# A decoder step on one core: mixer heads overlapped, memory projections moved forward, output projection restaged

## The chip, the core and the metric

The kernel runs on one core of a Trainium2 chip, as one program. A core has TensorE (PE in the profile; its weight loads are PEld), VectorE (DVE), ScalarE (ACT), GpSimd (POOL) and SyncE (SP), each with its own list of instructions worked off in order, and DMA queues that SP, ACT and POOL feed. SBUF holds the operands, PSUM takes the results of TensorE. Engines wait for each other by semaphores. The metric is the device time of one execution in microseconds (us).

## The reference, cut to what matters

One inference step of a one-layer decoder, all float32, for a prompt of 512 tokens and for 8 samples of one token each, width 1024:

```python
z = rms_norm(x) @ w_in                      # all projections at once
# group A, 4 heads of 128: mLSTM
s   = (q @ k.T) * exp(logd - m_t)           # decay
num = g_inter * (C @ q) + s @ v
den = g_inter * (n @ q) + sum(s)
h   = num / max(abs(den), exp(-m_t))
C_new = g_prev * C + (w_s * v).T @ k        # p_c; s_c for the samples
y_m = sigmoid(o) * rms_norm(h)
# group B, 4 heads of 128: sparse attention over the selected keys
y_a = softmax(q @ k_sel.T) @ v_sel
# memory: 256 tokens
mem_k = rms_norm(rms_norm(mem) @ w_ck);  mem_v = rms_norm(mem) @ w_cv
x = x + concat(y_m, y_a) @ w_out
q = rms_norm(rms_norm(x) @ w_cq)            # cross-attention
x = x + (softmax(q @ mem_k.T) @ mem_v) @ w_co
x = x + conv_ffn(rms_norm(x))               # up, conv, GELU gate, down
```

The samples take their state C (8 x 4 x 128 x 128), their keys and values (by page table) and their memory keys and values from caches.

## The kernel before, in words

**Products.** Each float32 product is made of three: weights and activations are split into a high part, as TensorE reads it, and the low rest. For every 128 output columns of weights (a tile) SP loads `raw` (512 KB), ACT casts it to `whi` (L831, or `act_split`), POOL subtracts to `wlo` (L845 and L1626, the low part), and PE runs high by high, high by low and low by high over eight k-blocks of 128. There are two slots `s`, for even and odd tiles; each buffer of a slot is free when the stage behind it is done (`raw_full`, `hi_full`, `split_full`, `w_used`, `out_free` are the semaphores, counted over all stages by `BASE`).

**Order.** Every engine's list is written out by hand, stage after stage: input projection, attention of the prompt, indexer of the samples, then the stretch that is changed here:

1. *Four mLSTM heads* (`pe_ml`, `act_ml`, `vec_ml`). For a head, PE spreads the running maxima over the partitions (`pe_ml_rows`), makes four score blocks (L1203), and numerator and denominator by key block (`pe_ml_nd`). ACT makes the decay of each block (L1268, L1270), DVE multiplies it in (L1309: 512, 384, 256, 128 columns). DVE makes the gate's column and `wv` (L1313, L1314), from which PE builds the new state; ACT copies it out (L1280, L1282) and stores it (`p_c`). DVE takes the denominator (L1321, L1322), ACT inverts it by log and exp (L1284, L1285), DVE makes `hb` (L1324), ACT squares it (L1289), PE sums over the head (L1245, a product with ones), ACT takes the root (L1292, L1293) and the output gate (`sg_e`, L1275 to L1277), and DVE scales by both (L1330, L1331: the two gate steps). Between these lie two samples' key products each head: PE spreads a sample's query row (L1058) into bank 2 or 3, DVE multiplies it with the gathered keys (L1065) and sums (L1069). All scores and sample rows go through the two banks 2 and 3; `p_c`, the maxima and the mean square through banks 0 and 1.
2. *The samples' softmax* (`satt_soft`, L1073 to L1102) and their gates (L1385 to L1411), small operations in turn.
3. *The state loop* over 8 samples b (`pe_mls`, `vec_mls`, `act_mls_store`, `sync_mls`). SP loads the state of b into one of two buffers `cb` once the store of b-2 has landed. PE spreads two rows of b (L1368), makes memory tile 2b (L912), the sample's attention value (`pe_satt_v`, L1112) and memory tile 2b+1. A memory tile is 128 columns of w_ck (tiles 0 to 7) or w_cv (8 to 15) over 256 memory tokens; `act_mem_tile` copies it out and casts the weights of two tiles on, PE transposes it back (`pe_mem_back`, L920). DVE updates the state, and ACT stores it (`out_s_c`). After the loop come the splits of y for the projection (`act_split_ml`, `vec_split_y`), the samples' mean square, and the sample part of y.
4. *Output projection* (`pe_out_proj`): x is transposed in (`pe_turn_in`), 8 tiles are made in pairs, each added to x by DVE (`vec_residual`, L1686). DVE normalises the memory keys (`vec_mem_norm`, four operations over all 2048 columns, with ACT's root between; L1731 and L1732 are the last two), PE transposes them (`pe_mem_keys`). ACT squares x (L1632), PE sums the squares (L249). `act_cache` starts 4 MB of cached memory keys and the stores of `p_mem_k` and `p_mem_v` from ACT's queue.
5. *Norm and query*: DVE writes the scaled x into one of two buffers `hs2`, ACT takes the high part from it, DVE the low part (L274), and PE starts the query tiles (`pe_fused`) k-block by k-block as the low parts come.

Behind that follow cross-attention, up, conv, down, which the change leaves alone. SP's order in the loop, which the change leaves as it is:

```python
for b in range(B):
    if b == 2: sync_reload(sp)
    if b >= 2:
        for t in (2 * b, 2 * b + 1): sp_weights(sp, t)
        sp.wait_ge(sc_stored[b % 2], 16 * (b // 2))
    else: sp.wait_ge(ym_ready, H)
    sp.dma_start(cb[:, b % 2], ...)          # state of sample b
```

and ACT's handing over of a memory tile: `act_mem_tile(t)` waits for PE's tile t, copies it to `kvT`, and then casts the weights of tile t + 2; `act_mem_step(t)` runs `act_mem_out` of t - 1 and `act_mem_tile` of t.

## Time and profile before

| what | value |
|---|---|
| median of 3 runs (lowest to highest) | 1365.85 us (1362.71 to 1368.11) |
| the profiled execution: its own time | 1363.25 us |
| its span in the profile | 1361.5 us |
| its mean granted clock | 0.90 |
| PE busy | 1139.3 us, 84% |
| DVE busy | 587.4 us, 43% |
| ACT busy | 486.0 us, 36% |
| POOL busy | 401.0 us, 29% |
| chain that ended last | PE 68%, DVE 15%, ACT 6%, issue 6%, DMA 2% |

The profile is of one execution; all its times are within the span, counted from the span's start. Busy time leaves out waits. The granted clock is TensorE's, as a part of full speed. The chain is followed back from the last instruction, at each step to what released it. "Issue" is time in which the engine waited for nothing that the profile shows. In the rows, a line is an operation with its start, its time, the line of the code, output and inputs, and in brackets how long its engine had been idle and what released it.

### The profile page before, as it was taken

What the parts mean: (1) busy time and instruction counts of PE and PEld (TensorE: products, weight loads), DVE (VectorE), ACT (ScalarE), POOL (GpSimd) and SP (SyncE); (2) the same over time, 40 slices, a digit from 0 to 9 for tenths busy, and PEclk for the clock granted to TensorE, in tenths of its full rate; (3) what the DMA queues carried; (4) which work ended last, traced back from release to release, by engine and by line L of the source; (5) the groups of instructions that cost most, each with busy time, mean ns of one, the idle gap of its engine ahead of it and who ended that gap; (6) DMA issues with size and microseconds to landing.
All of it is one profiled execution on the core that took longest, in us unless ns stands there. A gap on an engine that the chain in (4) does not pass through costs nothing.

```text
span 1361.5 us, 20030 instructions
## 1 busy us (share of the span) xinstructions
PE 1139.3 (84%) x7911; PEld 1000.9 (74%) x7911; DVE 587.4 (43%) x1105; ACT 486.0 (36%) x870; POOL 401.0 (29%) x200
## 2 busy tenths in 40 slices
PE   4788967657884586797687999988999999999998
PEld 4788857657873242686677986652999999998997
DVE  3405486886566566454513124552333334430000
ACT  5222242333244254123013454231355555543212
POOL 2212211122120112275121314540244444443442
PEclk9977788789897687799798999997899999999999
DMA  5223211113220112465161211844133332223222
GB/s 141 63 51 78 63 32 31 47 57 84 68 73 0 49 48 82 139 196 178 31 232 47 63 47 34 311 166 139 47 92 93 92 92 88 87 86 91 85 85 90
DMA packets 165331, 121.82 MB, mean 89 GB/s; under 512 B 7383, under 2 KB 154421, under 8 KB 164974
## 3 DMA queue, kind: packets, MB, share of 16 engines
q1 hardware_dynamic: 149536, 96.35, 23.6%
q10 hardware_dynamic: 12848, 14.08, 3.1%
q0 software_dynamic: 2880, 10.49, 2.7%
q8 instruction: 43, 0.70, 0.2%
q14 instruction: 24, 0.20, 0.0%
HBM read 111.81 MB, written 9.27 MB: 89 GB/s over the span
## 4 chain that ended last, share of the span: by engine, by line
PE 68%; DVE 15%; ACT 6%; issue 6%; DMA 2%; POOL 1%; ACTq 1%; DVEq 0%; POOLq 0%; SPq 0%
PE PS L237 43%; PE PS L912 3%; PE PS L1879 3%; PE PS L387 2%; DMA raw<-in_w_out 1%; PE PS L1368 1%; PE PS L2332 1%; ACT ikc L470 1%; PE PS L1839 1%; PE PS L1825 1%; DVE rw L314 1%; DVE tk L581 1%; PE PS L1112 1%; PE PS L953 1%; DVE tiny L580 1%
## 5 line engine op out<-in xcount | busy, mean ns | idle before, releaser
L237 PE MATMUL PS<-ahi,whi 128*128 128x260 f32 (+1 forms) x1456 | 311.9, 297 | 26.5 <-POOL wlo L2720 9.9
L1626 POOL TENSOR_TENSOR wlo<-raw,whi 128x1024 fp32r<-128x1024 f32 x84 | 201.0, 2393 | 415.9 <-ACT whi L831 415.9
L237 PE MATMUL PS<-alo,whi 128*128 128x260 f32 (+1 forms) x1456 | 302.1, 290 | 0.0
L237 PE MATMUL PS<-ahi,wlo 128*128 128x260 f32 (+1 forms) x1456 | 301.5, 290 | 0.0
L237 PEld LDWEIGHTS PS<-ahi,whi 128*128 128x128 f32 (+1 forms) x1456 | 235.1, 197 | 31.8 <-issue 18.1
L237 PEld LDWEIGHTS PS<-alo,whi 128*128 128x128 f32 (+1 forms) x1456 | 233.8, 196 | 0.0
L237 PEld LDWEIGHTS PS<-ahi,wlo 128*128 128x128 f32 (+1 forms) x1456 | 233.0, 195 | 0.0
L831 ACT CAST whi<-raw 128x1024 fp32r<-128x1024 f32 x108 | 113.1, 1048 | 317.0 <-PE PS L237 295.1
L2720 POOL TENSOR_TENSOR wlo<-raw,whi 128x1024 fp32r<-128x1024 f32 (+1 forms) x31 | 73.2, 2361 | 293.0 <-ACT whi L2758 293.0
L2459 DVE SCALAR_TENSOR_TENSOR PS<-ub,cw,PS 128x512 f32<-128x512 f32 x44 | 33.2, 755 | 156.0 <-ACT PS L2437 156.0
L237 PE MATMUL PS<-gHi,whi 128*128 128x260 f32 x352 | 71.1, 283 | 0.0
L237 PE MATMUL PS<-gHi,wlo 128*128 128x260 f32 x352 | 70.8, 282 | 0.0
L237 PE MATMUL PS<-gLo,whi 128*128 128x260 f32 x352 | 70.7, 282 | 0.0
L845 POOL TENSOR_TENSOR wlo<-raw,whi 128x1024 fp32r<-128x1024 f32 x18 | 43.1, 2394 | 61.2 <-ACT whi L831 61.0
L2551 DVE TENSOR_TENSOR xT<-xT,PS 128x520 f32 x8 | 5.6, 697 | 123.0 <-PE PS L237 123.0
L237 PEld LDWEIGHTS PS<-gLo,whi 128*128 128x128 f32 x352 | 54.3, 188 | 0.0
L237 PEld LDWEIGHTS PS<-gHi,whi 128*128 128x128 f32 x352 | 54.2, 188 | 0.1
L237 PEld LDWEIGHTS PS<-gHi,wlo 128*128 128x128 f32 x352 | 54.2, 188 | 0.0
L2758 ACT CAST whi<-raw 128x1024 fp32r<-128x1024 f32 (+1 forms) x31 | 32.1, 1037 | 57.3 <-PE PS L237 56.6
L1033 POOL DMA_INDIRECT skv<-in_cache_k,rowT x16 | 15.4, 962 | 102.1 <-DVE rowT L1021 55.3
L912 PE MATMUL PS<-hmhi,whi 128*128 128x256 f32 x128 | 38.6, 301 | 0.0
L912 PE MATMUL PS<-hmhi,wlo 128*128 128x256 f32 x128 | 37.2, 291 | 0.0
(502 smaller groups left out, 1870.7 us busy)
## 6 DMA issues: line engine op xcount, KB each, us to landing
raw<-in_w_up SPq DMA_DIRECT2D x44, 512.0 KB, 3.8
raw<-in_w_in SPq DMA_DIRECT2D x30, 512.0 KB, 3.8
ckv<-in_cache_mem_v SPq DMA_DIRECT2D x8, 1024.0 KB, 5.4
raw<-in_w_down SPq DMA_DIRECT2D x16, 448.0 KB, 3.8
raw<-in_w_ck SPq DMA_DIRECT2D x8, 512.0 KB, 4.5
raw<-in_w_cv SPq DMA_DIRECT2D x8, 512.0 KB, 4.3
raw<-in_w_out SPq DMA_DIRECT2D x8, 512.0 KB, 4.1
ckv<-in_cache_mem_k ACTq DMA_DIRECT2D x4, 1024.0 KB, 10.6
```

The lines of the kernel that those rows point to most:

```text
L237: ins = nc.tensor.matmul(out[0:m, half, 0:HALF], w[:, s, k, 0:m], x[:, k0 + k, half * HALF:(half + 1) * HALF], start=(first and k == 0 and ...
L314: V(nc.vector.tensor_tensor(t1[:, :, a], x[:, :, a], cos, ALU.mult))
L387: m = nc.tensor.matmul(bank[:, j:j + H], ikc[:, p0:p0 + 4, :].rearrange("d a r -> d (a r)"), iqS[:, :, b], start=True, stop=True)
L831: nc.scalar.copy(whi[:, s], raw[:, s]).then_inc(hi_full[s], 1)
L845: nc.gpsimd.tensor_tensor(wlo[:, s], raw[:, s], whi[:, s].bitcast(F32), ALU.subtract).then_inc(split_full[s], 1)
L912: m = nc.tensor.matmul(PJ[1][:, s, 0:NMEM], w[:, s, k, :], x[:, k, :], start=(k == 0 and j == 0), stop=(k == KT - 1 and j == 2))
L1033: nc.gpsimd.indirect_dma_start(skv[:, b % 2, t, :], None, table, bass.IndirectOffsetOnAxis(ap=rowT[:, t, b:b + 1], axis=0)).then_inc(skv_f ...
L1626: nc.gpsimd.tensor_tensor(wlo[:, s], raw[:, s], whi[:, s].bitcast(F32), ALU.subtract).then_inc(split_full[s], 1)
L1879: m = nc.tensor.matmul(PJ[o][:, half, 0:2 * P], w[:, k, o * P:(o + 1) * P], x[:, 4 * part + k, half * 2 * P:(half + 1) * 2 * P], start=(k ...
L2459: V(v.scalar_tensor_tensor(c, ub[:, s, r, 1:1 + SEQ], cw[:, 1, f:f + 1], c, ALU.mult, ALU.add))
L2720: g.tensor_tensor(wlo[:, s, :, 0:w], raw[:, s, :, 0:w], whi[:, s, :, 0:w].bitcast(F32), ALU.subtract).then_inc(split_full[s], 1)
L2758: a.copy(whi[:, s, :, 0:w], raw[:, s, :, 0:w]).then_inc(hi_full[s], 1)
```

## The change

Three edits in one. **Heads overlapped:** the next head's rows and first two scores stand ahead of this head's mean-square product on PE; on ACT the next head's gate column and first decay block stand ahead of this head's root, the output gate's three steps between the decay blocks, the copies of the state behind the denominator, and `p_c`'s store later still; on DVE the next head's first decay product stands ahead of this head's gate steps, and the sample's product apart from its sum. The sample rows move from banks 2 and 3 to PJ[1], with a semaphore of their own. **Memory tiles 0 to 2** go to the sample softmax and gates, the state loop starts with tile 3 and spreads the rest by a table; POOL's gathers and low parts follow the same order; the memory keys are squared on ACT in the turns of samples 4 and 5 and scaled on DVE in that of 6; the samples' attention value and root come earlier in the tail. **Output projection and norm:** the first half of the first output tile starts with the attention part of y as the low parts come; x is turned in in two halves with the first output tiles between; key transposes and squares stand in other places; the cache loads wait for the other slot; the norm has eight buffers; and PE runs the high products of both first query tiles ahead of the low ones.

The diff, cut to its core (waits and semaphores of moved code left out):

```diff
@@ pe_satt_k
-            nc.tensor.matmul(pe_bank(pe, 2 + b % 2)[:], rowsel[:, b, :], sw[:], ...)
+            if b < 2: pe.wait_ge(hm_lo, 4)
+            else:     pe.wait_ge(k_used, 2 * (b - 1))
+            nc.tensor.matmul(PJ[1][:, b % 2, :], rowsel[:, b, :], sw[:], ...).then_inc(k_row, 1)
@@ pool_mixers
-            for b in range(B):
-                for t in (2 * b + 2, 2 * b + 3):
-                    pool_weights(pool, t)
-                if b + 2 < B:
-                    pool.wait_ge(v_used, b + 1)
-                    gather("cache_v", b + 2)
+            for t in (2, 3, 4):
+                pool_weights(pool, t)
+            for b in range(2, B):
+                pool.wait_ge(v_used, b - 1)
+                gather("cache_v", b)
+                for t in (2 * b + 1, 2 * b + 2):
+                    pool_weights(pool, t)
+            pool_weights(pool, 17)
@@ pe_ml
             pe_ml_nd(pe, h, 0)
+            pe_satt_k(pe, 2 * h)
             pe_ml_score(pe, h, 2)
...
+            if h < H - 1:
+                pe_ml_rows(pe, h + 1)
             pe_satt_k(pe, 2 * h + 1)
             if h < H - 1:
-                pe_ml_rows(pe, h + 1)
+                pe_ml_score(pe, h + 1, 0)
+                pe_ml_score(pe, h + 1, 1)
             pe.wait_ge(hsq_ready, h + 1)
             nc.tensor.matmul(pe_bank(pe, 0)[:], ones[:], hsq[:], ...)
@@ act_ml, the new order
+            act_ml_decay(act, h, 1)
+            sg_e = exp(-z); sg_e = ln(sg_e + 1)
+            act_ml_decay(act, h, 2)
+            sg_e = exp(-sg_e)
+            act_ml_decay(act, h, 3)
+            dn = ln(dn); dn = exp(-dn)
+            cst = copy(bank 0); nst = copy(bank 1)
+            if h < H - 1: act_ml_m(act)
+            hsq = square(hb)
+            if h < H - 1: act_ml_em(act)
+            act.dma_start(O["p_c"][0, 0, h], cst[:, h % 2])
+            if h < H - 1: act_ml_first(act, h + 1)   # gate column, decay block 0
+            act_ml_root(act)
@@ vec_ml, the new order
+            vec_ml_decay(dve, h, 1); wcol, wv
+            vec_satt_k(dve, 2 * h)
+            vec_ml_decay(dve, h, 2); vec_ml_decay(dve, h, 3)
+            vec_satt_sum(dve, 2 * h)
+            dn (two steps); sg_s; hb
+            if h < H - 1: vec_ml_m(dve, h + 1)
+            vec_satt_k(dve, 2 * h + 1)
+            if h < H - 1: vec_ml_decay(dve, h + 1, 0)
+            vec_satt_sum(dve, 2 * h + 1)
+            y (two gate steps)
@@ pe_mls, act_mls_store
+        ROW_TILES = [(3,), (4, 5), (6, 7), (8, 9), (10, 11), (12, 13), (14,), (15,)]
-                pe_mem_step(pe, 2 * b)
+                pe_mem_step(pe, ROW_TILES[b][0])
                 pe_satt_v(pe, b)
-                pe_mem_step(pe, 2 * b + 1)
+                for t in ROW_TILES[b][1:]:
+                    pe_mem_step(pe, t)
...
-                for t in (2 * b, 2 * b + 1):
+                for t in ROW_TILES[b]:
                     act_mem_step(act, t)
+                if b in (4, 5):
+                    act_key_squares(act, b - 4)     # 4 squares, the root at 5
                 act.wait_ge(sc_in, b + 1)
                 act.dma_start(O["s_c"][0, b]..., cb[:, b % 2])
@@ vec_mls, vec_key_norm
+                if b == 6:
+                    vec_key_norm(dve)               # 8 products of 256 columns
@@ pe_mixers
+            pe.wait_ge(k_used, 2 * B)
+            pe_mem_step(pe, 0)
             pe_satt_soft(pe)
+            pe_mem_step(pe, 1)
+            pe_satt_turn(pe)
+            pe_mem_step(pe, 2)
             pe_mls(pe)
@@ act_mixers
+            act_mem_step(act, 1)
             act_satt_soft(act)
+            act_mem_step(act, 2)
             act_mls_first(act)
...
             act_mem_tile(act, 15)
+            act_satt_v(act)
+            act_mls_last(act)
             act_mem_out(act, 15)
             act_split_ml(act)
@@ pe_out_proj
+            pe_out_first(pe)       # half 0 over k = 4..7, 0..3 as y_lo comes, then half 1
+            pe_turn_in(pe, 0, 4)
+            pe_out_tile(pe, 0, 1)
+            pe_turn_in(pe, 4, KT)
+            for i in range(1, 4):
+                pe_out_tile(pe, i, 0)
+                for f in (2 * i - 2, 2 * i - 1):
+                    pe_sumsq(pe, 1, f, sq2, T)
+                if i == 3:
+                    pe_mem_keys(pe, 0, 4)
+                pe_out_tile(pe, i, 1)
+            pe_sumsq(pe, 1, 6, sq2, T)
+            pe_mem_keys(pe, 4, 6)
+            pe_sumsq(pe, 1, 7, sq2, T)
+            pe_mem_keys(pe, 6, KT)
@@ act_out_proj
             for i in range(4):
                 if i:
                     for f in (2 * i - 2, 2 * i - 1):
                         act_squares(act, 1, f)
+                act_split(act, 0, BASE["out"][0] + i + 1)
+                if i == 3:
+                    act_squares(act, 1, 6)
+                act_split(act, 1, BASE["out"][1] + i + 1)
                 if i == 1:
                     act_cache(act)
@@ act_cache
-            act.wait_ge(out_free[0], BASE["out"][0] + 1)
+            act.wait_ge(out_free[1], BASE["out"][1] + 1)
@@ pe_query_first, ahead of the loop of pe_fused, which now starts at n = 2
+            for k in range(KT):
+                pe.wait_ge(nhi_ready, KT + k + 1)
+                for s in range(2): for w in (whi, wlo): for half in range(2):
+                    nc.tensor.matmul(PJ[s][:, half, 0:HALF], w[:, s, k, :], ahi[:, k, ...], ...)
+            for k in range(KT):
+                pe.wait_ge(nlo_ready, KT + k + 1)
+                for s in range(2): for half in range(2):
+                    nc.tensor.matmul(PJ[s][:, half, 0:HALF], whi[:, s, k, :], alo[:, k, ...], ...)
```

## Rows read from the trace of the kernel before

**Rows 1.** Windows by stage: us, busy time of each engine (instructions), granted clock, DMA share, GB/s
```profile
459.30:540.40 81.10, 64.63 (x204) 31.34 (x203) 50.35 (x80) 41.36 (x80) 18.01 (x19) 0.84 0.24 68
540.40:553.20 12.80, 1.68 (x7) 1.25 (x7) 9.87 (x34) 0.81 (x3) 0.00 (x0) 0.50 0.61 209
553.20:637.60 84.40, 84.40 (x574) 71.77 (x574) 35.07 (x41) 24.04 (x45) 50.20 (x27) 0.94 0.55 169
637.60:691.00 53.40, 35.31 (x237) 32.79 (x236) 24.90 (x31) 8.67 (x18) 9.47 (x4) 0.78 0.15 43
691.00:730.20 39.20, 33.07 (x224) 30.18 (x224) 6.67 (x13) 6.39 (x9) 9.48 (x4) 0.91 0.61 215
730.20:755.70 25.50, 18.57 (x115) 16.34 (x116) 11.72 (x17) 11.93 (x20) 4.74 (x2) 0.93 0.14 41
```

**Rows 2.** Windows, two halves of the third head, DVE alone: us, busy, clock, DMA
```profile
502.70:514.59 11.89, 6.30 (x11) 1.00 0.18 51
514.59:522.01 7.42, 6.29 (x10) 0.54 0.24 70
```

**Rows 3.** Timeline of the third head: start, us, engine, line, operation
```profile
508.53 1.22 DVE L1065 TENSOR_TENSOR kprod<-skv,PS 128x1024 f32<-128x1024 f32 x1 [1.44 <-PE PS L1058]
509.90 1.22 DVE L1069 TENSOR_REDUCE tiny<-kprod 128x8 f32<-128x1024 f32 x1
...
512.40 0.69 DVE L1322 SCALAR_TENSOR_TENSOR dn<-PS,dn 128x512 f32<-128x512 f32 x1
...
514.59 0.69 DVE L1324 TENSOR_TENSOR hb<-PS,dn 128x512 f32<-128x512 f32 x1 [1.50 <-ACT dn L1285]
...
516.00 2.07 PE L1245 MATMUL PS<-hsq,ones 128*128 128x512 f32 x2 [2.31 <-ACT hsq L1289]
...
517.86 3.19 PE L1203 MATMUL PS<-z_m 128*128 128x512 f32 x4
```

**Rows 4.** Timeline, the gates' first operation, the first state row, and a cast
```profile
544.38 0.15 DVE L1385 TENSOR_TENSOR s<-gt,sm 8x4 f32<-8x4 f32 x1
...
553.16 3.78 PE L1368 MATMUL PS<-s_tok,rowsel 8*128 8x512 f32 x4 [1.68 <-DVE Qb L1411]
...
592.90 1.05 ACT L831 CAST whi<-raw 128x1024 fp32r<-128x1024 f32 x1
```

**Rows 5.** Timeline, the memory keys' last two operations and the output tile behind them
```profile
668.65 2.34 POOL L1626 TENSOR_TENSOR wlo<-raw,whi 128x1024 fp32r<-128x1024 f32 x1 [3.37 <-ACT whi L831]
669.12 4.02 DVE L1731 TENSOR_TENSOR mk_t<-mk_t,xc 128x2048 f32<-128x2048 f32 x1 [8.37 <-ACT xc L1744]
...
673.18 2.29 DVE L1732 TENSOR_TENSOR mk_t<-mk_t,ckg 128x2048 f32<-128x2048 f32 x1
...
676.65 0.77 PE L237 MATMUL PS<-ahi,whi 128*128 128x260 f32 x2 [9.21 <-DVE xT L1686]
```

**Rows 6.** Chain that ended last, pieces in order of time: start, us, what
```profile
556.94 5.42 PE PS L912 x24
...
584.53 2.92 PE PS L912 x24
587.45 1.91 PE PS L1368 x4
...
592.60 1.68 PE PS L1112 x16
...
694.62 17.27 DMA raw<-in_w_out
```

**Rows 7.** DMA issues in the state loop: output and input, queue, count, size, median us to land
```profile
raw<-in_w_cv SPq DMA_DIRECT2D x8, 512.0 KB, 4.3
out_s_c<-cb ACTq DMA_DIRECT2D x8, 256.0 KB, 5.1
```

**Rows 8.** Timeline, an ACT activation that also sums its row (cross-attention)
```profile
766.11 0.56 ACT L1956 ACTIVATE px<-PS,xc,rq 128x256 f32<-128x256 f32 x1 [1.33 <-DVE xc L2053]
```

**Rows 9.** DMA issues of the last turn, 632 to 640 us
```profile
out_s_c<-cb ACTq DMA_DIRECT2D x1, 256.0 KB, 2.9
```

More of the change, by code:

```diff
@@ L1291, in act_ml @@
                 act_ml_em(act)
-            S(a.activation(hrs[:], rd_bank(act, 0)[:], ACT.Ln, bias=epsc[:], scale=1.0 / DH), bank_read[0])
-            S(a.activation(hrs[:], hrs[:], ACT.Exp, scale=-0.5), hrs_ready)
+            act.dma_start(O["p_c"][0, 0, h], cst[:, h % 2]).then_inc(c_stored[h % 2], 16)
+            if h < H - 1:
+                act_ml_first(act, h + 1)
+            act_ml_root(act)
         def vec_ml_m(dve, h):
@@ L1534, in vec_mixers @@
             vec_mls(dve)
-            vec_satt_v(dve)
             dve.sem_inc(ya_ready, 1)
+            for h in range(H):
+                vec_split_y(dve, alo[:, h, 0:SEQ], z_m[:, 3 * H + h, 0:SEQ], ahi[:, h, 0:SEQ], H + h + 1)
             vec_split_y(dve, alo[:, 0:H, SEQ:T], z_m[:, 3 * H:4 * H, SEQ:T], ahi[:, 0:H, SEQ:T], 2 * H + 1)
@@ L1632, in act_squares, with pe_out_first @@
             nc.scalar.activation(sq2[:, f % 2], xT[:, f], ACT.Square).then_inc(sq_ready, 1)
-        def pe_out_proj(pe):
+        def pe_out_first(pe):
+            pe.wait_ge(split_full[0], BASE["out"][0] + 1)
+            pe.wait_ge(out_free[0], BASE["out"][0])
+            for half in range(2):
+                for n, k in enumerate((4, 5, 6, 7, 0, 1, 2, 3)):
+                    pe.wait_ge(y_lo, Y_PARTS if half else H if k >= H else H + k + 1)
+                    for j, (w, x) in enumerate(((whi, ahi), (whi, alo), (wlo, ahi))):
+                        m = nc.tensor.matmul(PJ[0][:, half, 0:HALF], w[:, 0, k, :], x[:, k, half * HALF:(half + 1) * HALF],
+                                             start=(n == 0 and j == 0), stop=(n == KT - 1 and j == 2))
+            m.then_inc(w_used[0], 1)
@@ L1700, in act_norm, with pe_turn_in @@
                 nc.scalar.copy(hi[:, k, 0:width], hs2[:, k % 2, 0:width]).then_inc(nhi_ready, 1)
-        def pe_turn_in(pe):
+        def pe_turn_in(pe, k0, k1):
             pe.wait_ge(x_in_s, 16 * (NTT + 1) + 16 * 6)
-            for k in range(KT):
-                bank = pe_bank(pe, 2 + k % 2)
+            if k0 == 0:
+                bank = pe_bank(pe, 2)
+                for k in range(KT):
+                    m = nc.tensor.transpose(bank[:, k * B:(k + 1) * B], xs_re[:, k * P:(k + 1) * P], ident[0:B, 0:B])
+                m.then_inc(bank_full[2], 1)
+            for k in range(k0, k1):
+                bank = pe_bank(pe, 3 - k % 2)
@@ L1737, in vec_mem_keys @@
+        def vec_mem_keys(dve, f0, f1):
+            v = nc.vector
+            for f in range(f0, f1):
                 V(v.tensor_scalar(mkT[:, f], rd_bank(dve, 2 + f % 2)[:, 0:NMEM], gains[:, G_CQ + f % 2:G_CQ + f % 2 + 1], SCALE_C,
@@ L1739, in vec_mem_keys, with pe_mem_keys @@
                 dve.sem_inc(kn_ready, 1)
-        def act_mem_keys(act):
-            act.wait_ge(ck_ss, 1)
-            S(nc.scalar.activation(xc[:, 0:8], xc[:, 0:8], ACT.Ln, bias=epsc[:], scale=1.0 / (2 * DH)))
-            S(nc.scalar.activation(xc[:, 0:8], xc[:, 0:8], ACT.Exp, scale=-0.5), ck_rstd)
-        def pe_mem_keys(pe):
+        def pe_mem_keys(pe, f0, f1):
             pe.wait_ge(mk_ready, 1)
-            for f in range(KT):
+            for f in range(f0, f1):
                 bank = pe_bank(pe, 2 + f % 2)
@@ L1887, in pe_co, with pe_query_first @@
             m.then_inc(w_used[s], 1)
+        def pe_query_first(pe):
+            for s in range(2):
+                pe.wait_ge(split_full[s], BASE["cq"][s] + 1)
+                pe.wait_ge(out_free[s], BASE["cq"][s])
+            for k in range(KT):
+                pe.wait_ge(nhi_ready, KT + k + 1)
+                for s in range(2):
+                    for w in (whi, wlo):
+                        for half in range(2):
+                            nc.tensor.matmul(PJ[s][:, half, 0:HALF], w[:, s, k, :], ahi[:, k, half * HALF:(half + 1) * HALF],
+                                             start=(k == 0 and w is whi), stop=False)
+            for k in range(KT):
+                pe.wait_ge(nlo_ready, KT + k + 1)
+                for s in range(2):
+                    for half in range(2):
+                        m = nc.tensor.matmul(PJ[s][:, half, 0:HALF], whi[:, s, k, :], alo[:, k, half * HALF:(half + 1) * HALF],
+                                             start=False, stop=(k == KT - 1))
+                    if k == KT - 1:
+                        m.then_inc(w_used[s], 1)
         def pe_fused(pe):
             base = BASE["cq"]
-            for n in range(KT):
+            pe_query_first(pe)
+            pe.wait_ge(kn_ready, KT)
+            pe.wait_ge(bank_read[1], filled[1])
+            for n in range(2):
+                pe_slot(pe, n)
+            for n in range(2, KT):
                 s = n % 2
@@ L2615, in act_tail @@
             act_mixers(act)
-            act.wait_ge(stores, 16 * 8)
             act.wait_ge(sv_stored, 16)
```

226 lines of the change are left out of this document (120 added, 106 removed).

## Prediction

> **What bounds the kernel now.** I read the stage table first, then the timeline of the heads, then the chain of waits behind them. The change touches the stretch from 459 to 756 us, 296 of 1361.5. In [rows 1] the reader is to see where TensorE (PE) idles there: 16.5 us in the heads, 11.1 in the sample softmax and its gates, 18.1 between the loop and the fourth output tile, 6.1 in the last four and 6.9 in norm and queries; only the state loop has none. What follows 755.7 is unchanged and I carry it over at its length.
>
> **1. Four heads.** One head takes 19.3 us, from its second decay product (384 wide, L1309) to the next head's. It has two halves, 11.89 to the start of `hb` (L1324) and 7.42 from there; DVE is busy 6.3 in each [rows 2].
> - The first half: DVE runs that product (0.6), the gate column and `wv` (0.9), the sample product (1.35), two decay products (0.75 and a 0.2 wait for ACT), the sample sum (1.45) and the denominator (1.45): its 6.3 of [rows 2], and 0.4 of gaps and wait; ACT's log and exp add the 1.50 for which `hb` waits [rows 3]. So `hb` starts at 8.25: 3.65 gained, mainly because the sample product comes ahead of the last two decay products and no longer waits 1.44 for PE [rows 3], and the gate's column no longer stands there.
> - The second half grows. The copies of the state now stand behind the denominator on ACT, so the next head's row products (0.95 each) start after them and `mb` comes at 10.15 where it lay beside `hb`. On PE the mean-square product (L1245) is queued behind two row products (1.9), a sample row (0.9) and two score blocks (1.5). It ends at 13.8, the root at 15.25, the two gate steps at 17.1. The store of `p_c` (0.4 of issue) sits ahead of the first decay block on ACT and is counted.
>
> 17.1 against 19.3, three times, is -6.6. The last head has no successor: from its second product, at 522.01 by [rows 2], to the stage's end at 540.4 [rows 1] it took 18.4; now 13.6, so -4.8. Heads: **-11.4**.
>
> These PE durations are at the higher of the clock's two levels, 2.4 GHz. The first half had a granted clock of 1.00, the second, in which PE paused 2.31 ahead of L1245, 0.54, near the lower level of 1.2 [rows 2, 3]; two scores took 3.19 there and L1245 2.07 [rows 3], which I halve. If the 1.7 us pause that is left brings the lower level, the period is 18.8: heads -5.3. If ACT's copies slip beside DVE, -13. I take full clock, since PE's work now closes up.
>
> **2. Softmax to the first state row**, 540.4 to 553.2, 12.8 us [rows 1, 4]. Memory tiles 0 to 2 fill PE there. They cost PE nothing, but stand in queues: ACT's exponential waits behind a weight cast (1.05 [rows 4]), PE's transposes of the result behind tile 1, together +1.9. POOL's low parts (2.4 each) now run beside DVE's small operations. In [rows 5] a DVE product of two SBUF operands took 4.02 us beside one, its equal 2.29 after it. The third low part starts with the first of these gate operations and holds it 2.4. **+4.3**, bounds 0 and +7.
>
> **3. The state loop**, 84.4 us, PE busy throughout [rows 1]: a tile 2.9, rows 1.9, a sample value 1.7 [rows 6]. Three tiles fewer would be -9.5. But the tiles now run two ahead of the samples, and SP's queue still reads: two weight loads, state b, two weight loads. The load of weights 2b+2 stands behind state b, which waits for the store of b-2. A turn is then: store 5.1 to land and weights 4.3 [rows 7], which I take at 4.5 behind the state's load, with 0.6 to issue that load and 0.5 to the cast, both estimates: 10.7 where PE needs 10.0. ACT hands over the finished tile only behind the cast that waits for this load, so PE waits too. In samples 4 and 5 eight squares (0.75 each, an estimate from the 0.56 of the 256-wide activation with accumulator [rows 8], and 0.19 to read that out) and a root, 3.0 and 3.5 us, stand on ACT ahead of the store and lengthen two turns to 14.9 and 15.4. By turns: 11.1 for sample 0, then load to load 10.7, 10.7, 10.7, 14.9 and 15.4, then 6.3 to the end; from first row to last sample value 85.3. **+0.9**; bounds -9.5 (loads in time) and +5 (stores later).
>
> The key norm's eight products on DVE (some 0.46 each, an estimate from the 0.69 that 512 columns take [rows 3]) lie under these waits: free. Were they exposed, 3.7.
>
> **4. Loop end to fourth output tile**, 53.4 us [rows 1]. Gone are: the four full DVE passes over the memory keys (2.3 to 4.0 each), for which PE waited 9.21 [rows 5]; the wait for the sample's root before any output product; the full turn-in ahead of the tiles. What is left: 5.5 until the last low part of `y` (L1467), the half product 2.9, two turn-ins of four (3.5 each), three tiles of 5.75 and the sums 0.8: 33.4. **-20**; bounds -16 (clock down in the new pauses) and -23. POOL and SP are ahead here: the tiles' weights arrive during the loop's last turn.
>
> **5. Last four output tiles**, 39.2 us. Here 4 MB of cache and 2 MB of stores start at the end of the fourth tile, as before, and one weight load issued 3.6 later takes 17.27 to land [rows 6]. This stays: the gate on the loads moves to the other bank, but ACT gets there after the same cast. ACT then holds the squares of tiles 4 and 5 behind that cast. PE has 17.6 us of work until it needs them, waits to 22.7, does sums and four key transposes to 26.3 and the last tile to 33. **-6.2**; bounds -2 and -9.
> The row says 17.27. The Trainium skill ("DMA: Bandwidth & Descriptors", section "Queues, rings and completion order") has each DMA engine take turns between queues packet by packet; read as equal shares, this load would land in 5.6 us by an estimate from the page and the 4.3 of [rows 7], and the stage would be 5 shorter. The row differs and decides.
>
> **6. Norm and first two query tiles**, 25.5 us [rows 1]. One square instead of two behind the last tile: -3.0. Eight scaled copies without waits let both query tiles run their high products while DVE writes; the low ones follow. Both end at 16.5 to 19 instead of 25.5. But both weight slots come free at once, so the third tile waits for a cast and a low part, 3.6: PE goes on at 20.1 to 22.6. **-4.2**; bounds -1 and -6.
>
> **Sum**: -11.4 + 4.3 + 0.9 - 20 - 6.2 - 4.2 = -36.6. Against this execution's own 1363.25 that is 1326.7; it stood 2.6 below the median of 1365.85, so on a median 1329. I say 1328.
>
> **Rivals.**
> - **The loop keeps PE's pace.** Loads then come in time and the loop gives its 9.5: 1328 - 10.4 = 1318. For it: the last store landed in 2.9 [rows 9], with which a turn would be under 10. Against: the median of 5.1 over all eight [rows 7]. 0.22.
> - **The heads overlap in name only.** The mean-square product waits behind the next head at the lower clock, heads -5.3: 1334. For it the 0.54 of [rows 2]; against, the shorter pause. 0.20.
> - **The load passes the cache traffic**, as by equal turns: 5 to 6 us less, 1322. Against it: the 17.27 of [rows 6] in the same place. 0.05. By the skill's rule above it would be this one.
> - **Slower: the clock stays down.** In the loop PE rests in every turn. If these rests hold the clock at half, as before the first row (3.78 for a row pair that takes 1.91, a tile then the 5.42 of the first against 2.9 [rows 4, 6]), 13 tiles cost 2.55 more and 8 row pairs 1.87: 48 us, giving 1376. It decides once rests cost over 37, three tiles in four at half. Against: most rests are under 1 us, and [rows 1] shows 0.94 here. 0.04.
>
> **How the numbers follow.** The forecast has 0.49 and is the likeliest. Within 0.5% (6.8 us, about what a measurement of this kernel can tell from no change) needs all gains but 4's to fail, or half the clock's loss. Faster 0.92, the same 0.04, slower 0.04. The best bounds together give 1303, the worst 1351; the range, cut to four in five, is 1308 to 1346 and takes in the first three rivals.
>
> **What would show it.** Heads: decay product to decay product near 17.1, L1245's successor at under 1 us. Softmax: first row 17 after the last gate step. Loop: a turn of 10.7 with SP waiting on the state's store, two turns of 15, PE idle there some 10 us. Output: no wait for the keys; the late weight load still at 17. Norm: third query tile 20 to 23 after the last output tile. I am wrong if the loop takes 75, if a head takes 19, or if what follows the queries changes length.

## The result, and the profile after

The changed kernel takes 1350.31 us (median of 4 runs, 1346.98 to 1352.43) against 1365.95 (1362.71 to 1368.11) on the same chip: ratio 0.9885, interval 0.9857 to 0.9914. It is faster, but by 15.6 us where 38 were forecast, and 1350 lies above the range. The profiled execution took 1349.98, span 1348.2; PE is busy 1146.0 us (85%), DVE 586.9, ACT 489.8, POOL 398.3, mean granted clock 0.897. Against the span of before that is -13.3, which the stages must add up to.

The stages of the changed kernel, by the window view (columns as in [rows 1]; stages as there, the last one to the first reduced scores):

```profile
459.10:542.70 83.60, 71.52 (x224) 36.75 (x224) 51.11 (x84) 41.38 (x80) 19.22 (x20) 0.84 0.23 66
542.70:559.70 17.00, 9.02 (x68) 7.76 (x66) 13.33 (x34) 3.72 (x8) 4.79 (x2) 0.84 0.70 219
559.70:646.00 86.30, 83.60 (x500) 69.19 (x501) 41.89 (x54) 26.12 (x60) 42.55 (x25) 0.83 0.54 158
646.00:683.10 37.10, 33.45 (x246) 31.81 (x247) 13.84 (x22) 8.75 (x16) 9.52 (x4) 0.91 0.21 61
683.10:717.40 34.30, 30.58 (x218) 28.50 (x217) 4.72 (x8) 6.94 (x9) 9.46 (x4) 0.90 0.68 245
717.40:750.30 32.90, 25.99 (x191) 24.78 (x190) 12.97 (x21) 15.11 (x26) 9.39 (x4) 0.95 0.16 49
```

The first line is to be read against 81.10 in [rows 1]: that window began at 459.3, two us behind the first row product of before (457.14), and with the same mark the heads took 83.2. The third line has three memory tiles fewer than [rows 1], but PE is as busy (83.60 against 84.40) and its granted clock is 0.83 against 0.94. Stage by stage, from the timelines:

| stage | before | after | difference | forecast |
|---|---|---|---|---|
| start of the heads | 457.1 | 459.1 | +2.0 | 0 |
| heads | 83.2 | 83.6 | +0.3 | -11.4 |
| softmax and gates | 12.8 | 17.1 | +4.3 | +4.3 |
| loop (before: with its last tile) | 84.4 | 86.3 | +1.8 | +0.9 |
| to the fourth output tile | 53.5 | 37.2 | -16.3 | -20 |
| last four output tiles | 39.1 | 34.3 | -4.8 | -6.2 |
| norm to the first reduced scores | 35.0 | 32.9 | -2.2 | -4.2 |
| the rest | 596.3 | 597.9 | +1.5 | 0 |

The start and the rest are code that the change leaves alone; over all traces below the start lay between 455.0 and 460.6 and the rest between 593.1 and 599.2. Heads of the same code took 83.5 or 85.8; the loop and the stage behind it, of the same code, took 86.3 and 37.2 (here) or 83.2 and 40.2 (n1_slot below), with nearly the same sum. So one stage of one profile says nothing under some 3 us.

So the heads, which should have given a third of the gain, gave nothing. The timeline of PE at the end of the second head shows it (start, us, line, operation, idle before):

```profile
492.75 1.03 PE L1248 MATMUL PS<-mk_tok,wcol 128*1 128x128 f32 x8
495.75 3.15 PE L1194 MATMUL PS<-rows,rowsel 4*128 4x512 f32 x4 [1.97 <-ACT cst L1309]
498.70 1.91 PE L1063 MATMUL PS<-sw,rowsel 8*128 8x512 f32 x2
500.54 3.35 PE L1213 MATMUL PS<-z_m 128*128 128x512 f32 x4
503.69 1.91 PE L1258 MATMUL PS<-hsq,ones 128*128 128x512 f32 x2
```

PE stands idle 1.97 for ACT's copy `cst`, which empties bank 0; then rows, a sample row, two scores and at last the mean-square product (L1258) run at half clock, 9.9 us in all. L1258 answers to L1245 in [rows 3], which waited for the square alone.

### The profile page after: what moved, and what is told of

Read it like the earlier page. It is cut to its first block, busy times and chain, and to the rows that moved or that the text cites. A ratio compares the mean times of both kernels' runs of the same rounds, so it can differ in the third digit from the quotient of the medians.

```text
span 1348.2 us, 20041 instructions
## 1 busy us (share of the span) xinstructions
PE 1146.0 (85%) x7911; PEld 1007.9 (75%) x7911; DVE 586.9 (44%) x1109; ACT 489.8 (36%) x886; POOL 398.3 (30%) x200
## 4 chain that ended last, share of the span: by engine, by line
PE 65%; DVE 15%; issue 9%; ACT 6%; DMA 2%; POOL 2%; ACTq 1%; DVEq 0%; POOLq 0%; SPq 0%
PE PS L237 42%; PE PS L1989 3%; PE PS L911 3%; PE PS L387 2%; ACT ikc L470 1%; PE PS L2461 1%; PE PS L1949 1%; PE PS L1935 1%; PE PS L1405 1%; PE PS L1213 1%; DVE rw L314 1%; POOL wlo L1697 1%; DVE tk L581 1%; PE PS L952 1%; DVE tiny L580 1%
## 5 line engine op out<-in xcount | busy, mean ns | idle before, releaser
L237 PE MATMUL PS<-ahi,whi 128*128 128x260 f32 (+1 forms) x1408 | 299.7, 295 | 15.5 <-POOL wlo L2841 9.9
L237 PE MATMUL PS<-alo,whi 128*128 128x260 f32 (+1 forms) x1408 | 291.2, 289 | 0.0
L237 PE MATMUL PS<-ahi,wlo 128*128 128x260 f32 (+1 forms) x1408 | 291.1, 289 | 0.0
L237 PEld LDWEIGHTS PS<-ahi,whi 128*128 128x128 f32 (+1 forms) x1408 | 226.1, 196 | 19.3 <-POOL wlo L2841 10.1
L237 PEld LDWEIGHTS PS<-alo,whi 128*128 128x128 f32 (+1 forms) x1408 | 225.0, 195 | 0.0
L237 PEld LDWEIGHTS PS<-ahi,wlo 128*128 128x128 f32 (+1 forms) x1408 | 224.7, 195 | 0.0
L2588 DVE SCALAR_TENSOR_TENSOR PS<-ub,cw,PS 128x512 f32<-128x512 f32 x44 | 33.2, 755 | 157.1 <-ACT PS L2566 157.1
L911 PE MATMUL PS<-hmhi,whi 128*128 128x256 f32 x128 | 42.4, 332 | 3.1 <-ACT mv_t L927 2.7
L911 PE MATMUL PS<-hmlo,whi 128*128 128x256 f32 x128 | 39.9, 312 | 0.0
```

The lines of the kernel that those rows point to most:

```text
L237: ins = nc.tensor.matmul(out[0:m, half, 0:HALF], w[:, s, k, 0:m], x[:, k0 + k, half * HALF:(half + 1) * HALF], start=(first and k == 0 and ...
L911: m = nc.tensor.matmul(PJ[1][:, s, 0:NMEM], w[:, s, k, :], x[:, k, :], start=(k == 0 and j == 0), stop=(k == KT - 1 and j == 2))
L2588: V(v.scalar_tensor_tensor(c, ub[:, s, r, 1:1 + SEQ], cw[:, 1, f:f + 1], c, ALU.mult, ALU.add))
```

## Experiments

Sixteen kernels ran; all edits are to the changed kernel. Those without a ratio ran once and count by their stages. The stages of each (from its timeline, marks as above, the loop to its last attention value, which was at 81.3 before with 56.6 behind it); of runs with an interval, the ratio to the kernel before. The 87.2 in two expectations ends the loop 0.9 later.

| kernel | heads | softmax | loop | to 4th | last 4 | norm | own time, ratio |
|---|---|---|---|---|---|---|---|
| changed | 83.6 | 17.1 | 86.3 | 37.2 | 34.3 | 32.9 | 1350.3, 0.9885 |
| h0_undone | 83.3 | 17.1 | 83.3 | 38.2 | 33.9 | 34.4 | 1345.1, 0.9877 |
| h1_copies | 74.1 | 17.9 | 83.7 | 38.7 | 33.6 | 35.3 | 1337.9, 0.9821 |
| h2_square | 87.6 | 17.8 | 84.9 | 38.2 | 33.6 | 34.4 | 1347.1 |
| h12_both | 74.1 | 17.9 | 84.0 | 38.6 | 33.4 | 32.9 | 1333.8 |
| t0_tiles | 83.5 | 12.8 | 81.1 | 40.7 | 33.5 | 32.8 | 1342.8, 0.9871 |
| u3_third | 85.9 | 12.8 | 81.0 | 40.7 | 33.5 | 32.8 | 1343.1, 0.9835 |
| l1_late | 85.8 | 17.1 | 79.0 | 38.5 | 33.2 | 32.8 | 1342.9 |
| l2_split | 85.8 | 17.1 | 85.2 | 41.7 | 34.5 | 34.3 | 1355.7 |
| l3_order | 83.5 | 17.1 | 79.1 | 38.5 | 33.4 | 32.9 | 1342.2 |
| c1_two | 83.5 | 14.9 | 83.9 | 38.8 | 34.6 | 34.4 | 1345.1 |
| s1_pool | 83.5 | 16.9 | 83.5 | 40.4 | 34.6 | 34.4 | 1352.8 |
| s2_rows | 85.8 | 13.7 | 85.2 | 38.7 | 33.7 | 32.9 | 1348.7 |
| o1_cache | 85.8 | 17.1 | 86.3 | 37.2 | 28.4 | 34.5 | 1346.1 |
| n1_slot | 83.5 | 17.1 | 83.2 | 40.2 | 34.4 | 31.2 | 1347.6 |
| b2_all | 76.4 | 14.2 | 81.1 | 38.5 | 28.4 | 32.8 | 1326.8, 0.9712 |
| b3_two | 77.2 | 13.7 | 79.3 | 38.1 | 28.4 | 30.0 | 1322.6, 0.9700 |

### Heads: the copies, the place of the product, or the clock

```diff
 h1_copies, act_ml
-            ln, exp of dn
             cst = copy(bank 0); nst = copy(bank 1)
+            ln, exp of dn
```

> Of the changed kernel, one thing moves: ACT's two copies of the head's state (cst, nst) go back ahead of the log and exp of the denominator, where they stood before the change. Heads are counted from the first row product to the end of the last gate step, 83.4 us in the changed kernel against 81.1 before. Theory A (the copies hold the next head's row products, since both use banks 0 and 1, and with them the sample row, the two scores and the mean-square product behind them): the rows start some 3 us earlier, under the denominator, scores are done before the square is ready, a period falls from 20.5 to 16 or 17, heads 70 to 74, time 1337 to 1341. Theory B (the place behind the scores alone makes the mean-square product late): rows move, the product still ends behind two scores, periods 19.5 to 20.5, heads 81 or more. Theory C (TensorE's lower clock level in this stretch, whatever the order): periods stay near 20.

Heads 74.1, periods 18.3, 16.8 and 16.7 where the changed kernel had 20.6, 21.8 and 19.0 and the kernel before 19.2 and 19.3; ratio 0.9821 (0.9778 to 0.9865). PE at the same place of the head:

```profile
488.82 1.03 PE L1248 MATMUL PS<-mk_tok,wcol 128*1 128x128 f32 x8
489.78 1.98 PE L1194 MATMUL PS<-rows,rowsel 4*128 4x512 f32 x4
491.60 1.02 PE L1063 MATMUL PS<-sw,rowsel 8*128 8x512 f32 x2
492.55 1.77 PE L1213 MATMUL PS<-z_m 128*128 128x512 f32 x4
494.16 1.02 PE L1258 MATMUL PS<-hsq,ones 128*128 128x512 f32 x2
```

The same five operations close up without a pause and at full clock. Theory A holds: the rows waited for the banks that the copies empty. The clock was a consequence: with the wait gone the four groups behind it take 5.4 us, for 9.9. The interval of the ratio still touches that of the changed kernel, but the 9.5 of the stage is far outside its scatter.

```diff
 h2_square, pe_ml
             pe_satt_k(pe, 2 * h + 1)
+            wait hsq_ready; mean-square product
             if h < H - 1:
                 pe_ml_score(pe, h + 1, 0); pe_ml_score(pe, h + 1, 1)
-            wait hsq_ready; mean-square product
```

> Of the changed kernel, PE's mean-square product goes ahead of the next head's two scores, and stays behind the rows and the sample row. Theory A (copies hold the rows): the product is 3.2 earlier, but the rows are as late, and DVE's first decay product of the next head now waits for a score behind it; a period falls by 1 to 2, heads 77 to 81. Theory B (its place behind the scores): a period falls by 3 to 4, heads 71 to 75. Theory C (clock): near 20 a period.

> Both: copies ahead of the denominator, mean-square product ahead of the two scores. Theory A: as with the copies alone within 1 us a head, heads 68 to 74 (the scores would have been done in time, so their place adds little). Theory B: as with the product's place alone, 71 to 75 where the copies alone give 81. Theory C: 80 or more.

With the product's place alone, periods were 24.1, 22.0 and 20.1: no gain, against both theories' numbers (the order of the changed kernel gave 20.6, 21.8 and 19.0, in other traces 24.4, 20.1 and 19.0). Its chain of waits in the third head (start, us, what) shows the product first, but DVE's decay product (L1332) now behind the scores that follow it:

```profile
517.30 1.95 PE PS L1194 x4
519.25 1.40 PE PS L1063 x2
520.66 2.01 PE PS L1255 x2
522.66 1.72 PE PS L1213 x2
524.48 0.70 DVE dd L1332
```

With both, heads are 74.1, as with the copies alone. Theory B falls.

> The changed kernel with the order of the heads as before the change on PE, ACT and DVE; the sample rows stay in PJ[1] and the two other changes stay. If the heads' overlap costs time, as the stage rows say (83.4 against 81.1): heads 80 to 82, time 1346 to 1349, and all of the gain comes from the two other changes. If the overlap is worth something that shows later (the stage boundary is drawn wrong): heads and what follows up to the first state row longer than 100.4 in sum, time over 1353.

Heads 83.3, time 1345.1, ratio 0.9877 (0.9837 to 0.9917), level with the changed kernel. (The 80 to 82 expected start from the 81.1 of [rows 1], which leaves out the first 2.2 us.) As changed, the overlap is worth nothing that can be measured.

### The memory tiles and the loop

```diff
 t0_tiles: ROW_TILES = [(2 * b, 2 * b + 1) for b in range(B)], no tile ahead, POOL's old order
 u3_third: t0_tiles and h0_undone
```

> The changed kernel with memory tiles 0 to 2 back in the state loop, two a sample, and POOL's list as before the change; heads, key norm and output projection stay changed. If the tiles' move gains (forecast: loop 9.5 shorter in work, 4.3 longer softmax): without it the softmax stage is 12.5 to 13.5, the loop to the last sample value 81 to 84 (8 turns of 10, the first slower), softmax and loop together 94 to 97 against 103.3 in the changed kernel with its clock at half for 36 us of the loop, and the time falls by 4 to 8, to 1342 to 1346. That is what the stage rows say. If the low clock comes of the heads or of the key squares, whatever the tiles do: loop 88 to 92, time 1350 or more.

> The changed kernel with the order of the heads and the place of the memory tiles as before the change: only the third part (output projection, norm, and the key norm it rests on) is left. Each of the two, undone alone, left the ratio at 0.987 to 0.988. If the third part gives all of the gain: heads 83, softmax 12.8, loop 81, to the fourth output tile 39 to 41, ratio 0.984 to 0.989, time 1340 to 1346. If the first two parts gain something together (the heads' end meeting the tiles): ratio over 0.991.

Without the tiles' move the softmax is 12.8 and the loop 81.1: together 9.5 less, of which 3.5 come back ahead of the output tiles, as one tile then stands behind the loop: up to the fourth output tile the tiles' move costs 6.0. The ratio, 0.9871 (0.9833 to 0.9908), is not apart from that of the changed kernel. With the heads undone as well it is 0.9835 (0.9803 to 0.9868): the third part alone, with the sample rows in PJ[1] and the sample values earlier in the tail, gives all that the whole change gives.

Three tiles fewer in the loop were to give 9.5; two things eat that. One is a pause at sample 5. The chain of waits of the changed kernel there:

```profile
612.20 0.20 ACT md L1495
612.42 2.31 DMA out_s_c<-cb
614.74 0.37 SPq L1384
615.15 6.75 DMA raw<-in_w_cv
...
623.39 5.46 PE PS L911 x24
```

Key squares (L1495), store, state load's issue, weight load, and a tile at half clock behind PE's pause.

```diff
 l1_late, act_mls_store            l3_order, sync_mls (b >= 2)
-  key squares for b in (4, 5)     -  weights 2b, 2b+1; state b
   store of state b                +  weights 2b+1, 2b+2; state b   (b = 2: 4, 5, 6)
+  key squares for b in (4, 5)
```

> Of the changed kernel, ACT squares the memory keys of samples 4 and 5 behind the store of that sample's state, not ahead of it. In the changed kernel the store of sample 4 was issued at 612.42, 2.2 us after the squares began, the weight load behind it landed 6.75 after its issue, and PE paused 2.69 from 620.7. Theory A (the squares hold the store, the store the load): the store leaves 2.2 earlier, the pause falls to 0.5 or less, and with it the half clock that followed it from 623.4 to 629; loop 82 to 85 where it was 87.2. Rival (the load is late for itself, beside gathers and the store): the pause stays over 2, loop 86 to 88.

> The changed kernel with SP's list shifted: one weight load more ahead of each state load (4, 5, 6, state 2, 7, 8, state 3, ...). Theory A (from the prediction: the load behind the state load, which waits for a store, paces the loop): the pause at sample 5 and the load's lateness go although the squares still hold the store; loop 79 to 83. Rival (in most turns PE sets the pace at 10.0, and only the squares of samples 4 and 5 make a load late; the rest of the loss is the clock): only the one pause goes, with some 3 us of half clock behind it, loop 80 to 84; both turns of half clock at its start stay. They differ in turns 1 to 4, which Theory A makes shorter than 10 nowhere and equal to 10.0 everywhere, the rival leaves as they are (13.1, 10.0, 10.0, 10.0).

Either edit takes the pause away: sample 5's turn is 10.0 where it was 15.3, loops 79.0 and 79.1. The other turns stay as they were in both (10.7, 13.1, 10.0, 10.0, 10.0), so PE sets the pace there and not the loads. From the heads' end to the fourth output tile it is then 134.6 in both, as in t0_tiles (134.5): without the pause the tiles' move costs nothing, and gains nothing.

The other is the clock. The window view of the changed kernel's second turn (third number from the right is the granted clock):

```profile
567.00:569.00 2.00, 2.00 (x16) 2.00 (x15) 0.00 (x0) 0.20 (x1) 0.00 (x0) 0.74 0.31 100
569.00:571.00 2.00, 2.00 (x15) 1.74 (x16) 0.00 (x0) 1.39 (x3) 0.28 (x1) 1.00 0.78 226
571.00:573.00 2.00, 2.00 (x4) 0.30 (x2) 1.33 (x2) 0.00 (x0) 1.67 (x3) 0.62 0.79 221
573.00:575.00 2.00, 2.00 (x10) 1.96 (x10) 1.97 (x2) 0.00 (x0) 2.00 (x1) 0.50 0.63 209
...
577.00:579.00 2.00, 2.00 (x15) 2.00 (x14) 0.34 (x1) 0.30 (x2) 0.00 (x0) 0.68 0.76 230
```

PE is busy throughout, yet the clock rises to 1.00 (2.4 GHz), falls to 0.50 and rises again. What PE did at 569 to 573 is the attention value (16 products of one column) and the next sample's rows, with no tile between.

```diff
 l2_split, turns of one tile       c1_two
-  tile; attention value           -  ROW_TILES = [(3,), (4, 5), ...
+  half tile; value; half tile     +  ROW_TILES = [(2, 3), (4, 5), ...
                                   -  tile 2 behind the softmax
```

> Of the changed kernel, in the three turns with one memory tile (samples 0, 6, 7) PE makes the attention value between the two halves of the tile, where it stood behind the tile and right ahead of the next sample's rows. In the changed kernel the clock fell to 0.50 from 571 to 578 and from 636 to 643, each time after an attention value (16 products of one column) with the rows right behind it, while PE was never idle; before the change a tile stood between. Theory A (that sequence brings the lower level): the clock stays at 1.00 there, the two stretches shorten by 3 to 4 us each, loop 79 to 82 where it was 87.2. Rival (the lower level comes from the pause ahead of the first row and of the late load, whatever stands in the turn): the clock falls again in these places, loop 86 to 88.

> The changed kernel with memory tile 2 in the loop's first turn, beside tile 3, instead of ahead of the first state row; tiles 0 and 1 stay in the softmax. Theory A (the second fall of the clock, 571 to 578, comes of the first attention value running straight into the next rows, with no tile between): the clock rises once, some 9 us after the first row, and stays at 1.00 until sample 5; second turn 10.0 to 10.3 where it was 13.1, first turn 13 to 14 where it was 10.7; loop 85 to 88 with a tile more in it. Rival (a second fall comes some 10 us after the first rise whatever stands there): falls again, second turn 12 or more.

Halving the tile failed in the first turn: the clock, at its lower level, did not rise for 21 us, from 561 to 582, and the turn took 12.9; late in the loop, where it was at 1.00, it stayed there from 634 to 650. With two tiles in the first turn it rises once and holds to 610:

```profile
564.00:566.00 2.00, 2.00 (x12) 2.00 (x12) 0.56 (x1) 0.00 (x0) 0.00 (x0) 0.59 0.79 236
...
568.00:570.00 2.00, 2.00 (x19) 1.98 (x19) 0.00 (x0) 0.64 (x2) 1.55 (x1) 1.00 0.41 131
...
572.00:574.00 2.00, 2.00 (x7) 0.76 (x6) 0.89 (x2) 1.52 (x3) 1.62 (x2) 1.00 0.96 278
```

The second turn is 10.0, as Theory A says. It is not a rule, though: in h12_both the changed kernel's own list of turns kept 1.00 from 554 to 575. What decides is open.

### Softmax, output, norm

```diff
 s1_pool, pool_mixers              s2_rows: s1_pool, and in vec_mls
   pool_weights(pool, 2)           +  Qb = copy(bank 2); vw
+  pool.wait_ge(qm_ready, 1)          three operations on the normaliser state
   pool_weights 3, 4               -  Qb = copy(bank 2); vw
```

> Of the changed kernel, POOL waits with the low part of tile 3 until the gates' queries are made (qm). In the changed kernel DVE's first gate operation took 2.32 us beside that low part, 0.15 before the change. Theory A (the low part holds the small operation): it takes 0.15 to 0.2, from softmax to the first state row 14.5 to 15 where it was 17.0; operations behind qm may be held instead (up to 2). Rival (the 2.32 is a wait for something else, the two loads of the samples' normaliser and maximum): it stays at 2.3 and the stage at 17.

> The changed kernel with POOL's low part of tile 3 behind the gates' queries, and DVE's copy of the spread queries (Qb) ahead of the three operations on the normaliser state. With the low part alone moved, the hold moved from the first gate operation to one of those three (2.71 where it takes 0.68) and the first state row came no earlier. Theory A (whichever DVE operation of two SBUF operands starts beside a low part is held until that ends, and the path runs through it): now none on the path is held, the first row comes 4 to 5 earlier, the stage is 12 to 13 us where it was 17.05. Rival (PE or the spread product sets the first row): the stage stays above 15.

DVE and POOL in the softmax and gates, before (its first gate operation, 0.15, is in [rows 4]), in the changed kernel, and in s1_pool:

```profile
542.37 0.34 DVE L1099 TENSOR_SCALAR aw<-aw,tiny 32x257 f32<-32x257 f32 x1
```

```profile
544.87 2.40 POOL L844 TENSOR_TENSOR wlo<-raw,whi 128x1024 fp32r<-128x1024 f32 x1 [4.18 <-ACT whi L830]
...
545.70 1.71 DVE L1109 TENSOR_SCALAR sp_row<-sp_row,tiny 32x257 f32<-32x257 f32 x1
...
548.68 2.38 POOL L844 TENSOR_TENSOR wlo<-raw,whi 128x1024 fp32r<-128x1024 f32 x1 [1.41 <-ACT whi L830]
...
548.77 2.31 DVE L1423 TENSOR_TENSOR s<-gt,sm 8x4 f32<-8x4 f32 x1 [0.16 <-DVE tiny L1111]
```

```profile
550.21 0.15 DVE L1425 TENSOR_TENSOR s<-gt,sm 8x4 f32<-8x4 f32 x1 [0.16 <-DVE tiny L1113]
...
557.23 2.71 DVE L1449 TENSOR_TENSOR sn<-s_tok,s 8x512 f32<-8x512 f32 x1
```

The hold goes with the low part: the first gate operation is back at 0.15, and a normaliser operation takes 2.71 in its place, so the stage stays at 16.9. In c1_two, where that low part has left the stage, the gate operation takes 0.15 and the stage 14.9, 2.2 less. In s2_rows the stage is 13.7, but not for the hold alone: of the 3.4 less, 1.2 is the three normaliser operations gone from the path, on which they stood before the change too. The longer operation ahead (1.71 in the changed kernel) is still held there, for 1.70, so the 12 to 13 expected was missed. The Trainium skill (SBUF — State Buffer, "SBUF: two separate sides") says that of a GpSimd operation and a DVE operation with two SBUF inputs the one that starts first holds a shared pair of ports for its whole instruction, and the other waits. The trace agrees: the operation on 8x4 numbers ends at 551.08, POOL's low part beside it at 551.06.

```diff
 o1_cache, act_out_proj            n1_slot, pe_query_first
-  after i = 1: 4 loads, 2 stores  -  for k: low products of s = 0, 1
+  one load per tile from i = 1,   +  for s: low products of k = 0 to 7
+  both stores behind the last
```

> The changed kernel with the four loads of cached memory keys and the two stores of the prompt's memory keys and values spread over the last four output tiles and behind them, one at a time, where ACT issued all six together after the fourth tile. In the changed kernel the one weight load behind them came 14.05 us late for ACT's cast. Theory A (6 MB ahead of it on the same DMA engines): that wait falls under 3, from the fourth to the last output tile 29 to 32 where it was 34.3. Rival (the query stage pays it back): the norm stage is longer by as much, 35 or more.

> Of the changed kernel, PE runs the low products of the first query tile for all eight k-blocks ahead of those of the second. In the changed kernel both weight slots came free together at 736.7, and the third query tile waited for a cast and a low part until 740.5. Theory A (that wait sets when PE goes on): the first slot comes free some 2.3 earlier, third tile 1.5 to 2.5 earlier, from the last output tile to the first scores reduced 30.5 to 31.5 where it was 32.9. Rival (the load of the third tile's weights or the low parts on DVE set it): 32.5 to 33.

ACT's casts of the late weights in the changed kernel, then of the same tile in o1_cache:

```profile
704.09 1.04 ACT L830 CAST whi<-raw 128x1024 fp32r<-128x1024 f32 x1 [14.05 <-DMA raw<-in_w_out]
```

```profile
698.59 1.05 ACT L830 CAST whi<-raw 128x1024 fp32r<-128x1024 f32 x1 [6.43 <-PE PS L237]
```

The cast now waits for PE and not for the load; the last four tiles take 28.4 (5.9 less) and the norm 34.5 (1.6 more, within its scatter): some 4 us gained in all, Theory A. In n1_slot the third query tile starts 21.4 us behind the last output tile's sum (740.14 less 718.77) where it was 23.0 (740.52 less 717.48), and its wait for the low part is 1.92 where it was 3.58: the shared release of the slots was part of it.

### All repairs

> All repairs in one: copies ahead of the denominator, mean-square product ahead of the scores, low part of tile 3 behind the queries and Qb ahead of the normaliser state, key squares behind the store, one weight load more ahead of each state load, cache loads one at a time, first query tile's low products first. By the single runs: heads 74, softmax 14 to 15, loop 78 to 81, to the fourth output tile 38 to 39, last four 28 to 30, norm to first scores 31 to 34, the rest 596: 1318 to 1326, ratio 0.966 to 0.972. If the repairs give the time back in the next stage (clock after shorter pauses, loads that meet): 1328 or more.

> As with all repairs, and memory tile 2 in the loop's first turn. If the second fall of the clock is there without it: 2 to 4 us less than with all repairs alone in turn two, 3 more in turn one; even, within 2 us of it. If the clock holds without it, as it did where the heads were repaired: 2 to 3 us more.

b2_all: 1326.8 us, ratio 0.9712 (0.9676 to 0.9747), the ratio within what the single runs promised, at its upper end, and the time just above. b3_two: 1322.6, 0.9700 (0.9669 to 0.9731). Their difference is inside the intervals; both beat the kernel before and the changed one. Their heads, 76.4 and 77.2, are above the 74.1 of the copies alone, mostly in the first period (20.4 and 20.8 for 18.3); why is open. The windows of b3_two:

```profile
456.20:533.40 77.20, 70.34 (x228) 35.71 (x227) 51.09 (x84) 41.35 (x80) 19.16 (x20) 0.85 0.24 69
533.40:547.10 13.70, 5.13 (x39) 4.30 (x37) 9.31 (x32) 2.03 (x5) 2.40 (x1) 0.78 0.66 225
547.10:626.40 79.30, 78.94 (x524) 66.04 (x524) 42.83 (x52) 26.65 (x60) 44.96 (x26) 0.93 0.59 181
626.40:664.40 38.00, 32.46 (x247) 30.74 (x247) 15.47 (x28) 9.69 (x18) 9.51 (x4) 0.96 0.21 62
664.40:692.90 28.50, 27.93 (x219) 26.92 (x218) 4.75 (x9) 6.87 (x9) 9.54 (x4) 1.00 0.69 222
692.90:722.80 29.90, 24.30 (x190) 23.12 (x189) 12.93 (x21) 15.21 (x26) 9.39 (x4) 1.00 0.38 124
```

PE's clock is 1.00 through the last two stages and 0.93 in the loop (0.83 in the changed kernel).

## Why the prediction was wrong

The direction was right, the size was not, and one step carries half of the miss (11.7 of 23.3). 1350 is where the prediction's worst bounds together lay (1351), which its range had cut off.

**1. Heads, -11.4 forecast, +0.3 measured: the step that failed.** The prediction counted the copies ahead of the row products, left a pause of 1.7 for PE, and still took full clock behind it, "since PE's work now closes up". The pause came (2.23, 1.97 and 1.97 us), and the clock fell: rows, sample row, two scores and mean-square product took 7.0, 9.9 and 7.0 us, where they take 5.4 at full clock (h1_copies). In the second head the product so ended 18.9 after the second decay product, for 13.8. Periods were 20.6, 21.8 and 19.0 for 17.1, against before +3.5 over three; the last head gained 3.2 of its 4.8. The rival "in name only" had the lower clock, at too small a price (18.8 a period). The first half was right in the second and third head: 8.7 for 8.25. With the copies early (h1_copies) periods of 16.7 to 18.3 lay around the forecast's 17.1.

**2. Softmax, +4.3: right in size, half by luck.** The hold of the gate operation by the third low part came as said (2.16 longer; s1_pool and c1_two). The +1.9 for two queues came another way: ACT's exponential starts at 544.81, 0.03 after DVE had its input ready, and PE's transposes wait for DVE and not for tile 1. In its place stand 1.05 for sums that queue behind tile 0 on PE, and a second hold, by the second low part (1.71 for 0.34, in the rows above).

**3. Loop, +0.9 forecast, +1.8 measured: near by luck.** The turns that the prediction lists add up to 79.8 and not to its 85.3. Turns of 10.7 from load to load were wrong: turns three to five are 10.0, PE's own pace. The store's median is 2.4 in this loop:

```profile
out_s_c<-cb ACTq DMA_DIRECT2D x8, 256.0 KB, 2.4
```

The 5.1 of [rows 7] belonged to the old order (5.0 in t0_tiles); with 2.4 the prediction's own sum is 8.0 a turn, under PE's 10.0. The squares of a sample took 2.2 for 3.0 and made one turn long (15.3), not two; in s1_pool two were (13.7 and 12.2). What the price of the loads was to take, the clock took: 0.50 for most of the first 20 us, where the kernel before had 0.50 for the first 10, and again at 623 and 636. So the rival on PE's pace was right on the loads, and the one of the clock right in kind, at a part of its price.

**4. To the fourth output tile, -16.3 for -20**, at the bound given for "clock down in the new pauses": PE waits 2.80 for the last low parts of y and runs the next 6 us at 0.50 (first row). With the loop it is -14.5 for -19.1, which is steadier than the two parts.

```profile
650.73 0.58 PE L1713 MATMUL PS<-ahi,whi 128*128 128x260 f32 x1 [2.80 <-DVE alo L1528]
...
740.52 0.48 PE L237 MATMUL PS<-ahi,whi 128*128 128x260 f32 x2 [3.58 <-POOL wlo L1697]
```

**5. and 6. -4.8 for -6.2 and -2.2 for -4.2**, inside their bounds. The late load took 17.1 where 17.27 was forecast; the third query tile came at 23.0, just past the 20.1 to 22.6, and its wait for a low part (second row above) was 3.58 for 3.6.

**Rivals.** The 0.05 for a load that passes the cache traffic was well placed: it did not pass. The prediction read the Trainium skill's rule ("DMA: Bandwidth & Descriptors", section "Queues, rings and completion order") as equal shares. The DMA view of 683 to 706 in the changed kernel suggests why that was a misreading:

```profile
q10 hardware_dynamic: 1632, 6.29, 71.2%
q1 hardware_dynamic: 2097, 1.06, 15.3%
...
raw<-in_w_out SPq DMA_DIRECT2D x1, 512.0 KB, 17.1
```

ACT's queue moved 6.29 MB in 1632 packets, 3.9 KB each, SP's 1.06 MB in 2097, 0.5 KB each: turns packet by packet, as the rule has it, would give ACT's queue some 7.6 times the bytes, if these packets are those of the rule. That it holds here was not tested by itself.

## What to carry to other kernels

Work of the next iteration that is moved ahead starts only when its buffers are free: follow each moved operation to the instruction that empties its bank, and move that one too. Here two copies of 0.27 us decided over 9 us. A pause of PE is to be counted twice, with what follows priced at the lower clock too: here 2 us of pause cost up to 4.5 more behind it. In a queue worked off in order, nothing that can wait belongs ahead of a store on which a load depends, and large transfers that nobody waits for are best issued one at a time between those that are awaited.

## What had not been expected

The clock fell while PE was never idle, in a stretch of one-column products and row products (571 to 578). Where it was low, and half tiles stood between such products, it stayed low for 21 us; that the one made the other is not shown, and the changed kernel's list of turns behaved otherwise in h12_both.

That a POOL operation holds a DVE operation of 8x4 numbers had been forecast. New was that an operation with one tensor and one column of scalars (L1109) is held as well, while the reciprocal just ahead of it, beside the same low part, took its usual 0.15, and that moving the low part only chose another victim.
